# Shifting the split weights by 16 and 48 words inside their buffers

## What is computed

```python
# first block, layer i (twice)
xn = rms_norm(h, attn_norm[i])
gq, gk, gv, gr, glr, fq, fk, fv, ff = split(xn @ w_in[i])
o_gla = silu(gr) * rms_norm(gla_chunk_causal(gq, gk, gv, ...))   # gated linear attention
o_fox = rms_norm(forgetting_attention(fq, fk, fv, ...))          # softmax attention with decay
h = h + concat(o_gla, o_fox) @ w_out[i]
h = h + conv_ffn(rms_norm(h, ffn_norm[i]), w_up[i], ..., w_down[i])

# second block (once)
q, k, v, qi, ki, wi, cu, cb, cc, ga, gb = split(rmsnorm(h) @ w_in_2)
y_attn = dsa_attention(q, k, v, qi, ki, wi) @ w_attn_out_2       # top-k attention
y_conv = (cb * short_conv(cc * cu)) @ w_conv_out_2
h = h + (sigmoid(ga) * y_attn + sigmoid(gb) * y_conv) @ w_out_2
h = h + (silu(f @ w_gate_2) * (f @ w_up_2)) @ w_down_2
```

## Time and profile before

| | |
|---|---|
| median of 3 runs | 2213.65 us (2213.56 to 2213.66) |
| profiled execution, first to last instruction (span) | 2212.6 us |
| TensorE matmuls busy | 2187.9 us, 99% |
| TensorE weight loads busy | 2006.8 us, 91% |
| VectorE busy | 1423.7 us, 64% |
| ScalarE busy | 1069.1 us, 48% |
| DMA from and to HBM | 196 GB/s over the span |
| mean granted TensorE clock | 0.999 |

### The profile page before, as it was taken

One profiled execution on the slowest core, in us unless ns is written; L12 is line 12 of the kernel. 1 busy time (PEld: TensorE's weight loads), 2 busy tenths in 40 slices (PEclk: granted clock), 3 DMA queues, 4 the chain that ended last, 5 costly groups with the idle time before them and its releaser, 6 DMA issues.

```text
span 2212.6 us, 39479 instructions
## 1 busy us (share of the span) xinstructions
PE 2187.9 (99%) x15711; PEld 2006.8 (91%) x15711; DVE 1423.7 (64%) x2661; ACT 1069.1 (48%) x2027; POOL 148.2 (7%) x245
## 2 busy tenths in 40 slices
PE   9999999999999999999999999999999999999998
PEld 8799999999997899998899889978899888998997
DVE  5356689559744466887498567869444465863664
ACT  5356556347533465555377534232344444552652
POOL 4111111000000011100000010101000000000001
PEclk9999999999999999999999999999999999999999
DMA  6656678686335546664354273777512222443651
GB/s 209 181 150 163 185 198 234 190 243 177 128 94 155 162 114 168 182 184 149 123 175 157 81 188 101 204 196 216 148 66 67 67 95 92 152 159 120 184 168 51
DMA packets 104737, 336.15 MB, mean 152 GB/s; under 512 B 14966, under 2 KB 19036, under 8 KB 102252
## 3 DMA queue, kind: packets, MB, share of 16 engines
q1 hardware_dynamic: 90460, 227.30, 31.5%
q0 software_dynamic: 13376, 105.03, 20.4%
q10 hardware_dynamic: 720, 1.31, 0.2%
HBM read 331.46 MB, written 102.79 MB: 196 GB/s over the span
## 4 chain that ended last, share of the span: by engine, by line
PE 92%; DVE 4%; ACT 2%; issue 1%; DMA 0%; POOL 0%; SPq 0%; ACTq 0%; DVEq 0%; POOLq 0%
PE G L1485 55%; PE G L1522 17%; PE G L1601 7%; PE X L1522 3%; PE X L1822 1%; DVE wL L2499 1%; PE X L1909 1%; PE X L1774 1%; PE X L1798 1%; ACT wH L1962 1%; PE X L1893 1%; PE X L1561 1%; PE X L1878 1%; PE X L1485 1%; PE X L1865 0%
## 5 line engine op out<-in xcount | busy, mean ns | idle before, releaser
L1962 ACT ACTIVATE wH<-raw 128x512 fp32r<-128x512 f32 (+3 forms) x741 | 492.2, 685 | 436.2 <-PE G L1485 354.8
L2499 DVE TENSOR_TENSOR wL<-raw,wH 128x512 fp32r<-128x512 f32 (+3 forms) x741 | 555.9, 763 | 219.3 <-ACT wH L1962 216.4
L1485 PE MATMUL G<-aH,wH 128*128 128x264 f32 (+3 forms) x1744 | 445.6, 318 | 3.5 <-DVE aL L2512 2.8
L1485 PE MATMUL G<-aH,wL 128*128 128x264 f32 (+3 forms) x1744 | 427.4, 308 | 0.0
L1485 PE MATMUL G<-aL,wH 128*128 128x264 f32 (+3 forms) x1744 | 427.3, 308 | 0.0
L1485 PEld LDWEIGHTS G<-aH,wH 128*128 128x128 f32 (+1 forms) x1744 | 284.5, 188 | 23.5 <-DVE aL L2512 3.2
L1485 PEld LDWEIGHTS G<-aH,wL 128*128 128x128 f32 (+1 forms) x1744 | 282.8, 188 | 16.3
L1485 PEld LDWEIGHTS G<-aL,wH 128*128 128x128 f32 (+1 forms) x1744 | 283.1, 188 | 13.0 <-issue 0.2
L1522 PE MATMUL G<-seven,wH 128*128 128x256 f32 (+2 forms) x1152 | 213.1, 284 | 2.8 <-DVE wL L2499 1.5
L2660 DVE TENSOR_TENSOR hT<-G,hT 128x528 f32<-128x528 f32 (+1 forms) x83 | 58.0, 698 | 199.4 <-PE G L1485 199.1
L1522 PEld LDWEIGHTS G<-seven,wH 128*128 128x128 f32 x1152 | 177.9, 189 | 5.3 <-issue 2.9
(11 more groups left out here) (412 smaller groups left out, 3967.7 us busy)
## 6 DMA issues: line engine op xcount, KB each, us to landing
raw<-weights SPq DMA_DIRECT2D x179, 512.0 KB, 4.3
weight_sums<-weights POOLq DMA_DIRECT2D x72, 704.0 KB, 6.4
raw<-weight_sums SPq DMA_DIRECT2D x192, 256.0 KB, 3.0
raw<-weights SPq DMA_DIRECT2D x145, 256.0 KB, 2.9
raw<-weights SPq DMA_DIRECT2D x48, 704.0 KB, 4.2
weight_sums<-weight_sums POOLq DMA_DIRECT2D x24, 704.0 KB, 4.8
weight_sums<-weights POOLq DMA_DIRECT2D x24, 512.0 KB, 5.3
weight_sums<-weights POOLq DMA_DIRECT2D x24, 448.0 KB, 5.0
```

The costliest lines, as they stand in the source:

```text
L1485: done = e.matmul(m.pair(i)[0:M, bank, 0:n], a[:, k, 0:M], b[:, kx, lo - t0:lo - t0 + n], start=(k == 0 and c == 0), stop=(k == nk - 1 and ...
L1962: e.activation(m.high(i)[:, c], m.raw(i)[:, c], ACT.Copy).then_inc(s.w_hi, 1)
L2499: e.tensor_tensor(m.low(i)[:, c], m.raw(i)[:, c], m.high(i)[:, c].bitcast(F32), ALU.subtract).then_inc(s.w_lo, 1)
```

## The change

It moves the split weights of some tiles further into their slots. A new function `behind(i)` gives 48 words (192 bytes) for token-major tiles, 16 words (64 bytes) for tiles of 512 columns, and 0 for all others, for `seven` tiles and for the tile right behind a `seven` tile. `wH` and `wL` grow by 64 words each to hold it. So `wL` starts 256 bytes further on than before and everything allocated behind it 512 bytes further on; `aH`, `aL`, `raw` and `wH` stay where they are. `places()` now also marks only the words that a tile has, and not its whole slot; the older tiles that it finds to be overwritten are the same ones for each tile, and each engine's instructions stand in the same order with the same waits.

```diff
+BEHIND = 64
...
+def behind(i):
+
+    role = ROLE[i]
+    if role[0] == "seven" or i and ROLE[i - 1][0] == "seven":
+        return 0
+    if role[0] in TOKEN_MAJOR:
+        return 48
+    return 16 if parts_of(role) is REAL else 0
...
-    last, k = [-1] * (NW * WMAX), 0
+    last, k = [-1] * (NW * WMAX + BEHIND), 0
...
-            at, n = WMAX * (n % NW), n + 1
+            at, n = WMAX * (n % NW) + behind(i), n + 1
         place[i] = at
-        size = 512 if role[0] == "seven" else WMAX
+        size = SIZE[i]
...
-        self.wH = sb("wH", [128, NW * WMAX], F32R)
-        self.wL = sb("wL", [128, NW * WMAX], F32R)
+        self.wH = sb("wH", [128, NW * WMAX + BEHIND], F32R)
+        self.wL = sb("wL", [128, NW * WMAX + BEHIND], F32R)
```

## The result

| | before | after |
|---|---|---|
| median (5 runs each, side by side) | 2213.65 us | 2229.8 us (2229.62 to 2230.64) |
| ratio, 95% interval | | 1.0073 [1.0062, 1.0084] |
| span of the profiled execution | 2212.6 us | 2228.0 us |
| TensorE busy | 2187.9 us | 2204.7 us |

The account below looks back on a forecast made before the run. The prediction took TensorE's matmul rate as the bound; 7.8 and 2.2 us saved made 10.0 us off, from 2213.7 to 2203.6 us. The likeliest case's range was 2199 to 2209, the 8-in-10 range 2193 to 2216.

Parts of the forecast that it names:

- What bounds the kernel: Whole kernel: the rate at which TensorE's matmuls follow each other; TensorE busy 2187.9 of 2212.6 us, idle 24.7 us.
- That start addresses bear on the surcharge: 256-column streams: steps of 113.8 to 119.4 ns differ by start address, dearest where stream and weights start at the same byte.
- Rival A: 512-column matmuls: start addresses have no effect, surcharge stays 13.4 ns, time within 1 us of 2213.65; chance 0.15.
- That carries a saving from 256 to 512 columns: 512-column streams 64 behind: save the 5.6 ns seen at 256 columns, as the surcharge is paid once a weight load.
- 7.8 and 2.2 us saved: Moved tiles: 1390 streams 64 behind save 5.6 ns each, 1860 streams 192 past save 1.2 ns each.
- The split by half of 512: Moved streams: distance modulo 512 matters, 64 behind saving 5.6 ns and 192 past only 1.2 ns.
- C: All 3250 moved streams: the half of 512 doesn't matter, each gains 5.6 ns, 18.2 us in all, 2195.4 us; chance 0.17.
- The pattern of three: Undisturbed 512-column stretch: two `wH` loads 64 behind near 0.221 us, one `wL` load 192 past near 0.226.
- The distance to the load beside: All streams: the distance that counts is to the weights loaded beside the stream, for the following matmul; 3250 streams change.
- rival B: Stream's absolute start counts, not distance; only token-major tiles gain, 768 matmuls x 3.4 ns = 2.6 us, 2211.0; chance 0.10.
- D: 512-column streams out of step with their loads: one in four pays 13 ns, 10.6 us more, 2224; chance 0.13.
- Terms taken as nothing: `wL` shift against other streams 0, within 3 us; shifted ScalarE and VectorE accesses 0; growing `wH` and `wL` 0.

## Why the prediction was wrong

- **What bounds the kernel** was right: the loss is all in TensorE's step, its idle time fell by 1.4 us, and no other engine mattered.
- **That start addresses bear on the surcharge** was right, though they don't fix it alone. Rival A said that a start address has no effect, by what the Trainium skill says in "TensorE: Matmul & The Clock Gate", section "Step-by-step: what each phase is for": that loading the next weights takes nothing from the running matmul. This case's traces contradict that conclusion: the step went from 226.7 to 233.5 ns in tiles where only a start moved. Whether the read ports have a part in it, no run shows.
- **The step that failed**: "That carries a saving from 256 to 512 columns", with the reason that the surcharge at the level start is the same for both lengths. It nearly is (12.7 to 13.4 ns at 256 columns, 13.4 at 512), but that was one point of two curves. Away from level the 256-column curve falls to 11.1 or below, and the 512-column one rises to 20. The saving of 5.6 and 1.2 ns per matmul was a loss of 6.8 ns in undisturbed tiles, 5.2 on average over the 3,231. So the two terms of the sum, 7.8 and 2.2 us saved, had the wrong sign: the 512-column matmuls, nearly all that they cover, lost 16.9 us. At 256 columns the sign held: in the last tile 48 matmuls went from 119.7 to 117.9 ns and the last 17 from 119.4 to 113.8. That this is just the value of the earlier trace rows is partly luck, since the same tile showed both.
- **The split by half of 512** (64 behind against 192 past) had no part in it. At 512 columns both cost about 233, so C had this right and the sign wrong. The pattern of three that was forecast doesn't appear. By unrounded starts, `zH` tiles step evenly at 233 to 234 ns, and `m2H` tiles at 231 and 235 to 236 ns in turn, a cycle of two where the operands of the loop have a cycle of three; both have the mean of 233.5. At 256 columns the 113.8 of the earlier trace rows was one of two rhythms and not the mark of a distance modulo 512: with all products at that distance, both rhythms appeared.
- **The distance to the load beside** was a wrong picture, though it made no difference here, where all weights of a tile move alike.
- **Absolute address** (rival B) was out: 2213.86 with everything 64 bytes up.
- **The rival on the other side** (D) came nearest in sign, and in place: steps of 0.23 to 0.24 where 0.227 stood. It was priced as 13 ns on one stream in four, 10.6 us. It was 5 to 7 ns on each, 16, so the 2229.8 lies beyond D's 2224 as well. D's reason, a stream out of step with its loads, was not tested.
- **Terms taken as nothing** were so: the room and the shift of `wL` measured 0.0 us within 2 (the kernel with the room alone), and ScalarE and VectorE kept their busy times.

**What stays open.** Why the sign turns with the column count, and what puts a run of matmuls into one rhythm or the other. The runs show that it is not the absolute address, and not the operand (`mo` has either sign), and no threshold in columns shows between 256 and 512.

## What to carry to other kernels

Where TensorE is busy 99% of the time and each matmul has its own weight load, the start of the moving operand against that of the weights was worth 3% of each 512-column step here, and it must be measured with the very column count in use: what a 256-column product gains, a 512-column one can lose. One kernel in which each tile of a role stands at another offset gives the whole curve in one trace. Check then on the full set of tiles, since a step read off a dozen matmuls may be one of two rhythms.

## What the runs showed of the hardware that was not expected

- At 512 columns and a load for each matmul, the step is 226.7 ns level, 229 to 230 at 64 bytes ahead and about 233 (231.7 to 234.0) at any other distance tried, down to 16 bytes, with a period of 256 bytes.
- At 256 columns level is the dearest: 119.8 against 117.8. At 320 columns the distance makes no difference (13.3 to 13.4 ns surcharge, one trace), and at 448 the cheapest is 64 ahead.
- One load in three out of line with its neighbours costs more for each shifted load than three in three: 13 ns against 20 for the three together.
- Runs of identical matmuls at identical addresses hold one of two steps, 113.4 or 117.7 ns at 256 columns, 202.6 or 206.8 at 448 (one tile each). At 512 columns off level, some tiles step evenly at 233 to 234 ns and others at 231 and 236 in turn.
- Shifting the weights did not change the recorded length of their loads, 0.19 us; their busy time is 2006.8 us before and after.
